# Starting two output projections inside the last attention unit, with GpSimd splitting the finished tiles, and moving the sums of squares behind four filler steps

## The reference

```python
# layer 0 (the last mixer is stick-breaking attention, 12 heads of 64)
y = concat([rwkv, pool, stick_breaking]) @ w_out;      x = x + y
# layer 1
x = x + concat([o_a, o_b]) @ w_out_even
# layer 2 (forgetting attention, 16 heads of 128)
x = x + (forgetting_attention(q, k, v, log_f) * silu(z)) @ w_out_odd
```

## Time and profile before

| | |
|---|---|
| median of 3 runs | 3478.31 us (3476.17 to 3479.16) |
| the profiled execution: its time, its span | 3474.39 us, 3472.5 us |
| PE busy | 3218.1 us (93%) |
| DVE, ACT, POOL busy | 38%, 36%, 39% |
| mean granted clock of TensorE | 0.967 of full |
| DMA | 286 MB, mean 82 GB/s |

### The profile page before, as it was taken

How to read it: one execution, slowest core, us unless ns; L and a number is a source line. 1 busy time by engine, 2 the same in 40 slices (tenths; PEclk the granted TensorE clock), 3 DMA queues, 4 the chain that set the end, 5 groups by cost and what they waited for, 6 DMA issues and landing times.

```text
span 3472.5 us, 47346 instructions
## 1 busy us (share of the span) xinstructions
PE 3218.1 (93%) x18030; PEld 2437.6 (70%) x18030; DVE 1319.2 (38%) x1699; ACT 1237.5 (36%) x1675; POOL 1362.7 (39%) x645
## 2 busy tenths in 40 slices
PE   6999998989998988899998997998999999999898
PEld 5777776767776866465555775786777877877686
DVE  4556655233233133888883332313211111111212
ACT  3333333244444232444442443323333233333322
POOL 2222221332232454877772221345433333333242
PEclk9999998999999988899999998999999999999999
DMA  4211110222122423122223222242222222222243
GB/s 162 75 51 52 56 56 29 83 78 67 60 66 79 147 91 104 46 65 72 69 72 102 73 83 75 87 155 97 92 81 83 79 84 79 85 79 80 68 131 102
DMA packets 92996, 286.03 MB, mean 82 GB/s; under 512 B 9776, under 2 KB 14160, under 8 KB 92368
## 3 DMA queue, kind: packets, MB, share of 16 engines
q1 hardware_dynamic: 64512, 233.14, 21.5%
q10 hardware_dynamic: 28368, 51.20, 4.4%
HBM read 261.21 MB, written 23.09 MB: 82 GB/s over the span
## 4 chain that ended last, share of the span: by engine, by line
PE 67%; issue 19%; POOL 6%; DVE 4%; ACT 3%; PEld 1%; DMA 1%; ACTq 0%; PEldq 0%; POOLq 0%; DVEq 0%; SPq 0%
PE ps L288 16%; PE ps L290 15%; PE ps L289 15%; POOL w_lo L2314 4%; PE ps L1887 2%; PE ps L661 2%; PE ps L662 2%; PE ps L663 2%; POOL act_lo L460 1%; PE ps L1411 1%; PE ps L1879 1%; PE ps L1428 1%; PE ps L707 1%; PE ps L305 1%; PE ps L1586 1%
## 5 line engine op out<-in xcount | busy, mean ns | idle before, releaser
L2314 POOL TENSOR_TENSOR w_lo<-raw,w_hi 128x1024 fp32r<-128x1024 f32 x442 | 1078.5, 2442 | 2015.6 <-ACT w_hi L472 2014.0
L288 PE MATMUL ps<-act_hi,w_hi 128*128 128x512 f32 x2624 | 1039.5, 396 | 35.8 <-POOL w_lo L2314 21.5
L290 PE MATMUL ps<-act_lo,w_hi 128*128 128x512 f32 x2624 | 1026.7, 391 | 0.0
L289 PE MATMUL ps<-act_hi,w_lo 128*128 128x512 f32 x2624 | 1026.2, 391 | 0.0
L472 ACT ACTIVATE w_hi<-raw 128x1024 fp32r<-128x1024 f32 x442 | 465.9, 1055 | 811.3 <-PE ps L290 394.3
L288 PEld LDWEIGHTS ps<-act_hi,w_hi 128*128 128x128 f32 x2624 | 496.0, 189 | 178.4 <-issue 72.5
L290 PEld LDWEIGHTS ps<-act_lo,w_hi 128*128 128x128 f32 x2624 | 495.4, 189 | 105.3
L289 PEld LDWEIGHTS ps<-act_hi,w_lo 128*128 128x128 f32 x2624 | 496.3, 189 | 101.0 <-issue 0.7
L358 DVE TENSOR_TENSOR mix<-ps,arena 128x512 f32 (+1 forms) x48 | 33.2, 692 | 442.0 <-PE ps L290 399.4
L661 PE MATMUL ps<-act_hi,w_hi 128*128 128x512 f32 x384 | 158.0, 411 | 0.0
L933 PE MATMUL ps<-act_hi,w_hi 128*128 128x512 f32 x352 | 155.3, 441 | 0.0
(11 more groups left out here) (358 smaller groups left out, 4067.9 us busy)
## 6 DMA issues: line engine op xcount, KB each, us to landing
raw<-stream SPq DMA_DIRECT2D x442, 512.0 KB, 3.5
arena<-residual ACTq DMA_DIRECT2D x48, 256.0 KB, 2.7
residual<-mix ACTq DMA_DIRECT2D x32, 256.0 KB, 2.1
mix<-x ACTq DMA_DIRECT2D x4, 1024.0 KB, 9.7
residual<-arena ACTq DMA_DIRECT2D x4, 1024.0 KB, 5.9
kept_qk<-mix ACTq DMA_DIRECT2D x16, 256.0 KB, 2.3
arena<-kept_qk ACTq DMA_DIRECT2D x16, 256.0 KB, 3.4
out<-arena ACTq DMA_DIRECT2D x4, 1024.0 KB, 5.0
```

Of the source, the lines that this page charges most:

```text
L288: pe.matmul(dst, w_hi[:, slot, j, :], act_hi[:, kt, :], start=first, stop=False)
L289: pe.matmul(dst, w_lo[:, slot, j, :], act_hi[:, kt, :], start=False, stop=False)
L290: mm = pe.matmul(dst, w_hi[:, slot, j, :], act_lo[:, kt, :], start=False, stop=last)
L2314: nc.gpsimd.tensor_tensor(w_lo[:, s, :, :], src[:, s % 2, :, :], w_hi[:, s, :, :].bitcast(F32), ALU.subtract).then_inc(split_done, 1)
```

## The change

The diff, cut to its core:

```diff
-        def gemm_two(pe, n, ready, count, between=None):
-            if between is None:
+        def gemm_two(pe, n, ready, count, between=None, k0=0, k1=KT):
+            if between is None and k0 == 0:
                 pe.wait_ge(split_done, n * 2 + 4)
-            for kt in range(KT):
+            for kt in range(k0, k1):
...
+        EARLY = (KT - 1, 0, KT - 1)
         def out_tensor(pe, layer, n0, before):
             pe.wait_ge(evac_act, before)
-            gemm_two(pe, n0, mix_lo, KT * layer)
+            gemm_two(pe, n0, mix_lo, KT * layer, k0=EARLY[layer])
...
+        def mix_round(act, tiles):
+            for ft in tiles:
+                nc.scalar.activation(act_hi[:, ft, :], mix_tile(ft), ACT.Copy).then_inc(mix_hi, 1)
+        def mix_rest(pool, layer):
+            for ft in range(KT):
+                pool.wait_ge(mix_hi, KT * layer + ft + 1)
+                nc.gpsimd.tensor_tensor(act_lo[:, ft, :], mix_tile(ft), act_hi[:, ft, :].bitcast(F32),
+                                        ALU.subtract).then_inc(mix_lo, 1)
...
@@ sb_tensor, every unit
+                first.steps(4)
                 A.wait_before(pe, u)
                 S.mark(pe.matmul(ps[:, 5, :], head_ones[:], sq_q, start=True, stop=True), "sumq")
                 S.mark(pe.matmul(ps[:, 6, :], head_ones[:], sq_k, start=True, stop=True), "sumk")
-                first.steps(KT)
-                first.steps(2)
+                first.steps(KT - 2)
...
@@ sb_tensor, unit
                 after.steps(13)
+                if not more:
+                    pe.wait_ge(evac_act, N_OUT1)
+                    gemm_two(pe, N_OUT1, mix_lo, 0, k0=0, k1=6)
                 for h in range(2):
                     V.wait(pe, f"vb{h}", u)
...
                     S.mark(mm, f"tri{h}")
                 after.steps(4)
+                if not more:
+                    gemm_two(pe, N_OUT1, mix_lo, 0, k0=6, k1=10)
                 A.wait(pe, "w1", u)
...
                 S.mark(mm, "pv")
+                if not more:
+                    gemm_two(pe, N_OUT1, mix_lo, 0, k0=10, k1=KT - 1)
@@ sb_scalar, unit
                 take(u, 3)
+                if not more:
+                    mix_round(act, range(0, 6))
...
                     A.mark(..., f"l{h}")
+                if not more:
+                    mix_round(act, range(6, 11))
...
                     A.mark(..., f"w{h}")
+                if not more:
+                    mix_round(act, range(11, KT - 1))
@@ attention_tensor, unit
+                def early(k0, k1):
+                    if not more:
+                        if k0 == 0:
+                            pe.wait_ge(evac_act, N_OUT3 - at.shift)
+                        gemm_two(pe, N_OUT3, mix_lo, KT * at.layer, k0=k0, k1=k1)
...
                     fill(2 * h)
+                    early(0, 5)
                     V.wait(pe, f"sc{h}_3", u)
...
                     fill(2 * h + 1)
+                    early(5, 8)
                     A.wait(pe, f"pt{h}", u)
...
                 fill(3)
+                early(8, KT - 1)
@@ attention_scalar, unit
                 A.mark(..., "vn")
+                if not more:
+                    V.wait_before(act, u)
+                    mix_round(act, range(0, 5))
...
                     fill(2 * h)
+                    if not more:
+                        mix_round(act, range(5, 9))
                     S.wait(act, f"tp{h}", u)
...
                 fill(3)
+                if not more:
+                    mix_round(act, range(9, KT - 1))
@@ gpsimd
-            rests(4, 2 * (N_U + 2))
+            rests(4, 2 * (N_OUT1 + 2))
+            mix_rest(pool, 0)
+            rests(2 * (N_OUT1 + 2), 2 * (N_U + 2))
...
-            rests(2 * (N_F + 2), 2 * N_TILES)
+            rests(2 * (N_F + 2), 2 * (N_OUT3 + 2))
+            mix_rest(pool, 2)
+            rests(2 * (N_OUT3 + 2), 2 * N_TILES)
@@ scalar, after meet 3 (layer 0) and meet 9 (layer 2)
-            mix_split_scalar(act, 0)
+            mix_round(act, (KT - 1,))
@@ vector, after meet 3 and meet 9
-            mix_split_vector(dve, 0)
```

More of the change, by code:

```diff
@@ L2391, in _ @@
             meet(act, 9)
-            mix_split_scalar(act, 2)
+            mix_round(act, (KT - 1,))
             out_scalar(act, 2, N_OUT3)
@@ L2425, in _ @@
             meet(dve, 9)
-            mix_split_vector(dve, 2)
             out_vector(dve, 2, N_OUT3)
```

## The result

The changed kernel takes 3438.37 us (median of 4 runs, 3436.28 to 3443.36), against 3478.73 before in the same comparison: a ratio of 0.9883, interval 0.9865 to 0.9901. That is 40.4 us less. A second comparison gave 3440.88 against 3479.17, ratio 0.9893 (0.9877 to 0.991), 38.3 less. The profiled execution went from a span of 3472.5 us to 3435.2.

A forecast was written before the change was run, and what follows sets the result against it. PE, busy 93% of the span, was taken to bound the kernel, with time won only where it idles or runs at low clock. 18.2 + 9.0 + 5.0 = 32.2 us off 3478.31 gave 3446, range 3436 to 3459.

The forecast's parts named there:

- the better case: Last units: DVE gets the port first, gaps too short for the low clock; 38.7 us gained, 3440, chance 0.08.
- the likeliest case: Whole kernel: all three gains as summed, 3446 us, own range 3439 to 3453, chance 0.60.
- Part A: Stick-breaking unit starts: four filler steps fill a 2.31 us gap in five units, low clock goes in four; 18.2 us.
- clock not won: Low clock follows the unit starts or moves elsewhere; 22 us gained in all, 3456, chance 0.17.
- instruction supply at the loop's back edge: Filler directly after the loop edge exposes the jump, 42 us lost at four edges; 3488, chance 0.03.
- Part B: Last stick-breaking unit: early output projection steps bring the third output tile from 1106.0 to 1097.0, 9.0 us; bounds 4 and 12.5.
- the handover: Ahead of step 15 in both last units: PE's drain, an ACT copy and a POOL subtract, 2.6 us idle.
- the weight wait of the third tile: Last stick-breaking unit: residual loads, cast and POOL's rest follow ACT's copy, a new wait of 1.6 us.
- the 0.8 taken off: Each last unit: 0.8 us deducted for more changes between kinds of matmul and low clock behind idle gaps.
- Part C: Last forgetting unit: early output projection steps bring the third output tile sooner, 5.0 us; bounds 1 and 8.
- Transposes 2.4: Last forgetting unit: the transposes after the four scalings were priced at 2.4 us.
- the port: DVE and POOL take turns at a shared SBUF port, so adds, masks and the four scalings wait for POOL subtracts.

The follow-up runs named there:

- part A alone: Kernel before, with only four filler steps moved ahead of the sums of squares: 3461.01 us against 3479.56, ratio 0.9949.
- the kernel with one step: Kernel before, with only one filler step moved ahead of the sums of squares: 3470.64 us, run once, beside a median of 3480.12 before.
- the eight traces above: All profiled executions with the early output projection in the last stick-breaking unit: step 6 starts 24.04 to 24.06 us after z in each.
- the repeat: The changed kernel run and traced once more, nothing altered: 3440.88 us against 3479.17, ratio 0.9893.
- The run with VectorE's subtracts: Changed kernel with the subtracts of layer 2 on VectorE instead of GpSimd: single time 3438.89 us, beside 3480.12 before.
- the kernel without the meetings: Changed kernel without the waits of meetings 3 and 9, ScalarE waiting for the last unit's product instead: 3434.86 us against 3480.12, ratio 0.9871.
- the last kernel: Changed kernel without waits at the meetings, with VectorE's subtracts in layer 2 and GpSimd's last weight rest later in layer 0: 3431.75 us, ratio 0.9871.
- part B alone: Changed kernel with sums and layer 2 as before, so only layer 0's output projection begins early: 3468.56 us against 3479.56, ratio 0.9973.
- part C alone: Changed kernel with the stick-breaking stage as before, so only layer 2's output projection begins early: 3471.19 us against 3479.56, ratio 0.9977.

## Why the prediction was right, point by point

The forecast was 3446 us, 32.2 less than before; measured were 40.4 and 38.3 less. Both times (3438.37 and 3440.88) lie within the stated range of 3436 to 3459, but nearer to the better case's 3440 than to the likeliest case's 3446; the first is 0.6 us under the likeliest case's own range of 3439 to 3453. The signs and the waits are those of the likeliest case in all three parts, and the sizes of B and C were too small.

**Part A: 18.2 forecast, 18.5 measured.** The 2.31 us gap in five units and 1.65 of low clock in four were both right, and part A alone and the kernel with one step separate them: 6.5 us are the clock's. The unit starts are 61.1 apart, forecast 61.2. The rival "clock not won" fell for this part. So did the one of instruction supply at the loop's back edge: the sums follow the last filler matmul without a noted wait, and no unit is longer than another. (Its sum was also off: 42 us lost, against the 23 of the gains that it leaves, is 19 slower, not 10.)

**Part B: 9.0 forecast, 11.1 measured.** The first early step waits 3.05 us (3 forecast), from it to `tri` it is 9.86 (9.9, low clock included), steps 6 to 9 take 5.65 (5.4), p by v 2.3 (2.3). That the masks of head 1 decide when `tri` ends was in the prediction, and the eight traces above bear it out. These masks were ready 19.64 us after z (1053.08), where the sum had 20.5: their waits for POOL came to 2.0 us instead of 2.6, and the sum was 0.2 too long, since 1066.7 + 1.5 + 0.8 + 2.6 is 1071.6, not 1071.8. The low clock on the early steps came in this trace and not in the repeat, and cost nothing in either. Smaller than in the sum were also: the handover, 2.34 instead of 2.6; the weight wait of the third tile, 0.9 instead of 1.6, since ACT issued the loads beside its copy and began the cast 0.93 after the copy's start (the earlier trace rows could have told: the loads were issued at 1088.68, before the copies ended at 1089.15); and the 0.8 taken off, of which the changes between kinds of matmul took some 0.4 and a low clock nothing.

**Part C: 5.0 forecast, 8.8 measured.** This is where the term was mis-sized most. The step that failed is "Transposes 2.4": that is what they cost at clock 0.50, and I had corrected `tri` and p by v for the clock, but not these. At the full clock they took 1.07 up to the next matmul, 1.3 less. The second is the port: turns were forecast and do happen, but the scalings came to 4.84 us where the sum had 5.8, and PE stood still for 0.78, not 2.1; that is 1.1 less. The run with VectorE's subtracts shows that it is POOL's work that stretches the scalings. The Trainium skill (SBUF — State Buffer, two separate sides) had this as whole turns at a shared port, for a two-port mode as well. The runs agree for the scalings (one SBUF input, 1.28 alone, 4.84 beside POOL), for the add (1.49 alone, 3.42 beside a weight rest) and for the copy in the earlier trace rows. The rest, 1.4, is the handover (2.33 instead of 2.6), the weights of the third tile (0.5 less) and the 0.8 taken off, of which some 0.2 was spent.

**The handover and the weights** were the new waits that the prediction named. What they cost together, 2.7 us a layer, is shown by the kernel without the meetings.

**What the chances missed:** the better case (3440, 0.08) had A right and B and C at 12.5 and 8, 38.7 us in all. The two measured gains, 40.4 and 38.3, are of its size, but not for its reasons: DVE waits for the port (the masks took 2.79 us, the scalings 4.84), and the clock did fall in these units. So it is by several terms that were each too large by 0.3 to 1.3 us that the time came out near it. The prediction also looked for idle time only around the edited code: `tri` waited 1.0 us a unit for the masks in units 1 to 4 before (4.0 us over four of them), and still does.

## What to carry to other kernels

Price every matmul stretch of a chain that will no longer be interrupted at the full clock, each of them: the low clock in the trace of before is part of what filling the gaps wins (6.5 us of part A, and 1.1 of the 1.3 on ten transposes, by their durations). A short wait that costs the clock is worth more than its length: 0.68 us of work put into a gap of 2.31 won 2.0 per unit. When idle time ahead of a dependent step is filled, look for the chain that this step waits for as well, since in the last kernel the early steps began 1.8 us sooner and at the full clock, and all of it came back as waits of 2.26 and 0.75 at `tri`. A low clock or an idle stretch that lies beside such a chain costs nothing, so read from several traces what stays equal; and keep GpSimd's long instructions out of the stretches where VectorE works for that chain.

## What had not been expected of the hardware

The clock: with 1.47 us of noted idle time at a unit start it stayed high in all five. With 2.15 it fell in four of five, in each of the three traces that have this wait, and the unit that was spared was not the same one: by the unit starts 63.5 us apart it was the start at 766.48 before, at 899.18 with part B alone, and at 839.16 with part C alone. Behind the handover's 2.18 it fell in layer 2 (0.71 over 3.4 us) and not in layer 0 (1.00 over 5.8) in the first trace of the changed kernel, and the other way round in the second (1.00, and 0.71 in layer 0). Behind some 3.04 us ahead of the early steps it fell in the first (0.62 over 3.5 us) and not in the second (1.00). So one kernel has it in different places in different executions, and what decides is not shown here.

The copies in ACT's queue and its DMA issues overlap: the two residual loads were issued from 1072.60 on, at the start of the copy of tile 15, and the cast began at 1073.53, where the sum had put them one after the other.
